# Moving VectorE's LayerNorm rows inside the periods of a fast-algorithm FFN product

## Chip, cores and metric

One Trainium2 chip, all 8 cores. Each core computes one of the 8 batch elements by itself; nothing is exchanged between cores. The metric is the device time in microseconds (us) of the slowest core.

## What is computed

One encoder layer. The mixing sublayer (convolution, windowed attention, memory attention, a gated merge) ends in LayerNorm 1, and a SwiGLU network with LayerNorm 2 follows. Per core the sequence has 2048 tokens of 1024 channels, and the inner width of the network is 2816. What matters here:

```python
def layer_norm(x, g, b):
    mu = jnp.mean(xf, axis=-1, keepdims=True)
    var = jnp.mean(jnp.square(xf - mu), axis=-1, keepdims=True)
    return ((xf - mu) * lax.rsqrt(var + LN_EPS)) * g + b

x = layer_norm(DEEPNORM_ALPHA * x + merged @ w_o, ln1_g, ln1_b)
gate, up = jnp.split(x @ w_ffn_in, 2, axis=-1)
ffn = (jax.nn.silu(gate) * up) @ w_ffn_out
return layer_norm(DEEPNORM_ALPHA * x + ffn, ln2_g, ln2_b)
```

## The kernel before

Tokens go in 16 blocks of 128 (`tb`), in two passes of 8 blocks (`P`). Every engine runs its instructions in the order in which the program issues them, and waits for other engines by semaphore. There is no planner: the order is the order of the Python calls.

**The first FFN product** runs over 44 units (22 for each pass): `u` even is a gate unit (128 columns of the gate half), `u` odd the up unit that is multiplied with the gate of the unit before. Each unit is a 2 by 2 block product by a scheme with seven block products in place of eight. `f1_period(cur, prev)` is one period: it interleaves the early products of unit `cur` with the late ones of unit `prev`. A full period is seven products of four matmuls (`prod`, all recorded at L233), which I number:

1. of `cur`, copied out of PSUM by ACT (`t1`, L1163)
2. of `prev`, copied by ACT (`t3`, L1163)
3. of `cur`, added by DVE into `t1` (`c11`, L1166); if `cur` is an up unit, POOL then multiplies it with its gate (L1173)
4. of `prev`, added by DVE into `t3` (`c22`, L1166)
5. of `cur`, copied by ACT (`tu`)
6. of `prev`; if `prev` is a gate unit, ACT takes two SiLUs (L1169), else DVE (L1174) and POOL (L1173) take products
7. of `prev`, accumulated on top of product 4 in the same bank, which therefore waits until `c22` has read it; DVE then adds it into another buffer (`c12`, L1166)

At the end of a period DVE folds the weights of unit `cur + 2` (`fold_w1`, three instructions at L806 to L808), which SP loaded at the period's start (`load_w1`, 512 KB, from a cache in HBM), as soon as product 7 of the period before was done with the buffer.

**LayerNorm 1 of blocks 8 to 15** is interleaved with the first pass. `d_chain(t)` issues, for a handful of blocks in different stages: the store of the row that `d_Y` made one call before (`y_pend`, SP, 512 KB), transposes of block `t-4` on PE (`d_Tpe`, L1109), the sum of squares and small statistics of block `t` on ACT (L1023, L1082 to L1084) and POOL (L1086, L1037), the copy of the transposes by ACT, and DVE's two rows: `d_C(t-2)` (scale and offset, L1045) and `d_Y(t-1)` (centre and gain, L1041), each one pass over 128x1024 floats. It is called behind every even period `u` from 0 to 18, with `t = 10 + u//2`; rows of C come up to `t = 17`, rows of Y up to `t = 16`.

From `u = 8` on, POOL issues two loads of the second product's weights behind each period (`load_w2`, cast from float to bf16).

**The second FFN product** (`f2_block`) runs a block of 128 tokens at a time; behind each block comes LayerNorm 2: DVE's addition of the residual (L1284), ACT's sum of squares, three small DVE instructions, DVE's rows `ln_center` (L1041) and `ln_scale` (L1045), the store of the output on SP, and on SP again `load_hb(tb + 3)`, which waits until that store has landed. Block 7 is the last of the first pass; the early products of unit 22 run among its matmuls, and the periods 23 to 43 follow it.

Of the kernel before, what the change touches and what calls it, by code (L numbers as in the profile page):

```python
# [97 lines left out]
def _build(plan):  # L98
# [27 lines left out]
    out_d = nc.dram_tensor("out", [T, D], F32, kind="ExternalOutput").ap()  # L126
# [9 lines left out]
    sp = Eng(nc, nc.sync, "sp", plan)  # L136
# [8 lines left out]
    def dma(e, out, in_, slot, deps=()):  # L145
        e.wait(deps)
        e.eng.dma_start(out=out, in_=in_).then_inc(slot.sem, 16)  # L147
        slot.count += 16
        return slot.tok()
# [31 lines left out]
    rs16 = nc.alloc_sbuf_tensor("rs16", [128, 32], F32)  # L181
# [794 lines left out]
    e_state = {}  # L976
# [63 lines left out]
    def ln_center(buf, tab, k, deps):  # L1040
        return dve.run(lambda: nc.vector.scalar_tensor_tensor(  # L1041
            out=buf, in0=buf, scalar=mvt[:, k % 4, 0:1], in1=tab, op0=ALU.subtract, op1=ALU.mult), deps)

    def ln_scale(buf, dst, rs, tab, deps):
        return dve.run(lambda: nc.vector.scalar_tensor_tensor(  # L1045
            out=dst, in0=buf, scalar=rs, in1=tab, op0=ALU.mult, op1=ALU.add), deps)
# [42 lines left out]
    y_pend = []  # L1089
# [25 lines left out]
    def d_Tev(tb):  # L1115
        bT, t_tr = d_state.pop(("tr", tb))
        t_x1T[tb] = act.run(lambda: nc.scalar.copy(
            x1T[:, tb // 8, (tb // 4) % 2, :, (tb % 4) * 128:(tb % 4 + 1) * 128], psb[:, bT, :].rearrange("p (a b) -> p a b", a=8)), [t_tr])
        banks.release(bT, t_x1T[tb])
# [45 lines left out]
    def plus(buf, b, deps):  # L1165
        return dve.run(lambda: nc.vector.tensor_tensor(out=buf, in0=buf, in1=ps[:, b, :], op=ALU.add), deps)  # L1166
# [6 lines left out]
            return pool.run(lambda: nc.gpsimd.tensor_tensor(out=dst, in0=up, in1=gate, op=ALU.mult), deps)  # L1173
        return dve.run(lambda: nc.vector.tensor_tensor(out=dst, in0=up, in1=gate, op=ALU.mult), deps)  # L1174

    def f1_period(cur, prev, fill=lambda: None, part=None):
        new = cur is not None and cur not in unit
        if cur is not None:
            load_w1(cur + 2)
            P, i, up, W, A11, A12, A21, A22 = f1_operands(cur)  # L1180
            n = i % 2
            free = t_free.setdefault(("u",) if up else ("g", n), {})
        if new:
            s = unit[cur] = {"T": TU if up else [TG[n], TG[2 + n], TG[4], TG[5]]}
            s["x"], dx = banks.alloc(1)
            t = prod(s["x"], W, 0, A11, True, [dx, w1_tok[cur], t_x1T[8 * P:8 * P + 8]])
            s["t1"] = grab(s["T"][0], s["x"], [t, free.get("11"), tg0])
        if prev is not None:
            q = unit[prev]
            Pq, iq, upq, Wq, A11q, A12q, S3q, A22q = f1_operands(prev)  # L1190
            g = unit[prev - 1] if upq else None
            j1, j2 = actT[2 * iq], actT[2 * iq + 1]
            sa = sa_tok[Pq]
            t = prod(q["x"], Wq, 5, S3q, False, [q["tu"], sa[3]])
            q["t3"] = grab(q["T"][2], q["x"], [t, c_free[upq]])
        fill()
        if new:
            y, dy = banks.alloc(1)
            t = prod(y, W, 3, A12, True, [dy])
            s["c11"] = plus(s["T"][0], y, [t, s["t1"]])  # L1200
            banks.release(y, s["c11"])
            if up:
                gg = unit[cur - 1]
                a_tok[2 * i, 0] = times(actT[2 * i][:, 0:512], s["T"][0], gg["T"][0], [s["c11"], gg["g11"], e_state["dep"]])
                free["11"] = a_tok[2 * i, 0]
                t_free["g", n]["11"] = a_tok[2 * i, 0]
        if silu12:
            silu12.pop()()
        if prev is not None:
            z, dz = banks.alloc(1)  # L1210
            t = prod(z, Wq, 4, SA[:, 0], True, [dz, sa[1]])
            q["c22"] = plus(q["T"][2], z, [t, q["t3"]])
            fill()
        if part == "head":
            return
        if cur is not None and "tu" not in unit[cur]:
            s = unit[cur]
            t = prod(s["x"], W, 6, SA[:, 1], False, [s["t1"], sa_tok[P][2]])
            s["tu"] = grab(s["T"][1], s["x"], [t, free.get("12"), tg0])
            if not up:  # L1220
                s["g11"] = silu(s["T"][0], s["T"][0], [s["c11"]])
        if prev is not None:
            t = prod(q["x"], Wq, 1, A22q, False, [q["t3"]])
            if not upq:
                q["g22"] = silu(q["T"][2], q["T"][2], [q["c22"]])
                q["g21"] = silu(q["T"][3], ps[:, q["x"], :], [t, d_free[0]])
                banks.release(q["x"], q["g21"])
            else:
                a_tok[2 * iq, 1] = d_free[0] = times(j1[:, 512:1024], ps[:, q["x"], :], g["T"][3], [t, g["g21"], e_state["dep"]], dve)
                banks.release(q["x"], d_free[0])  # L1230
            fill()
            t = prod(z, Wq, 2, SA[:, 2], False, [q["c22"], sa[4]])
            w1_free[prev % 4] = [t]
            e_state["mm"] = t
            q["c12"] = plus(q["T"][1], z, [t, q["tu"]])
            banks.release(z, q["c12"])
            if not upq:
                def later12():
                    q["g12"] = silu(q["T"][1], q["T"][1], [q["c12"]])
                silu12.append(later12)  # L1240
            else:
                a_tok[2 * iq + 1, 1] = times(j2[:, 512:1024], q["T"][2], g["T"][2], [q["c22"], g["g22"], e_state["dep"]])
                c_free[0] = c_free[1] = a_tok[2 * iq + 1, 1]
                a_tok[2 * iq + 1, 0] = times(j2[:, 0:512], q["T"][1], g["T"][1], [q["c12"], g["g12"]])
                t_free["u",]["12"] = t_free["g", iq % 2]["12"] = a_tok[2 * iq + 1, 0]
        if cur is not None and part is None:
            fold_w1(cur + 2)
# [4 lines left out]
    def load_hb(tb):  # L1252
        if tb < 16:
            r = tb % 3
            hb_tok[tb] = dma(sp, HB[r], y_d[tb * 128:(tb + 1) * 128, :], hb_slot[r], [x1_st[tb], hb_free[r]])
# [24 lines left out]
    def f2_block(tb, hooks={}):  # L1280
        r = tb % 3
        bO, tk = f2_mm(tb, hooks)
        xb = HB[r]
        t_h = dve.run(lambda: nc.vector.scalar_tensor_tensor(  # L1284
            out=xb, in0=xb, scalar=ALPHA, in1=bank2(bO), op0=ALU.mult, op1=ALU.add,
            accum_out=hsum[:, 1, tb:tb + 1]), [tk, hb_x[tb]])
        banks.release(bO, t_h, 2)
        t_st2 = ln_stats(xb, [t_h], tb)
        t3 = ln_tiny(t_st2, tb, hsum[:, 1, tb:tb + 1], 0)
        t_rs2 = ln_rstd(t3, tb, rs16[:, 16 + tb:17 + tb])  # L1290
        t_y = ln_center(xb, ln2t[0], tb, [t3, e_state["ln2"]])
        t_ln = ln_scale(xb, xb, rs16[:, 16 + tb:17 + tb], ln2t[1], [t_rs2, t_y])
        hb_free[r] = [dma(sp, out_d[tb * 128:(tb + 1) * 128, :], xb, s_out[r], [t_ln])]
        load_hb(tb + 3)

    hb_x = {}

# [1 line left out]
        if tb < 16:  # L1299
            hb_x[tb] = ln_scale_ap(HB[tb % 3], rs16[:, tb:tb + 1], ln1t[:, 1, :], [hb_tok[tb], d_state["rs", tb]])  # L1300

    def d_chain(t, lo, hi):
        while y_pend:
            y_pend.pop(0)()
        if lo <= t - 4 < hi:
            d_Tpe(t - 4)
        if lo <= t < hi:
            d_S(t)
            d_small(t)
        if lo <= t - 4 < hi:  # L1310
            d_Tev(t - 4)
        if lo <= t - 2 < hi:
            d_C(t - 2)
        if lo <= t - 1 < hi:
            d_Y(t - 1)

    def f1_begin(u, second=False):
        f1_period(u, None, part="second" if second else "head")
# [15 lines left out]
            d_chain(tb - 6, 8, 16)  # L1334
    w2_order = list(range(22))
    for u in range(22):
        f1_period(u, u - 1 if u else None)
        if u % 2 == 0 and u < 20:
            d_chain(10 + u // 2, 8, 16)
        if u >= 8:  # L1340
            for _ in range(2):
                if w2_order:
                    load_w2(w2_order.pop(0))
# [18 lines left out]
    for P in range(2):  # L1362
        if P == 0:
            e_sums(1, [e_state["mm"]])
            for tb in range(3):
                load_hb(tb)
            hb_prep(0)
        for tb in range(8 * P, 8 * P + 8):
            if tb not in (7, 15):
                hb_prep(tb + 1)  # L1370
            f2_block(tb, {24: lambda: f1_begin(22), 8: lambda: f1_begin(22, True)} if tb == 7 else {})
            if tb in (1, 2):
                fold_w1(23 + tb)
        if P == 0:
            for u in range(22, 44):
                f1_period(u, u - 1 if u > 22 else None)
                if u == 32:
                    hb_prep(8)
            f1_drain(43, 8)
# [67 lines left out]
```

How the kernel before makes its waits and increments, by code:

```python
    def wait(self, deps):  # L45
        for tok in _flat(deps):
            if tok[0] == "E":
                _, src, v = tok
                k = id(src)
                if self.seen.get(k, 0) >= v:
                    continue
                self.seen[k] = v
                src.needed.add(v)
                if self.plan is not None:
                    self.eng.wait_ge(src.sem, src.vmap[v])
            else:
                sem, val = tok
                k = id(sem)
                if self.seen.get(k, 0) >= val:
                    continue
                self.eng.wait_ge(sem, val)
                self.seen[k] = val
# [1 line left out]
    def run(self, fn, deps=(), inc=True):  # L64
        self.wait(deps)
        ins = fn()
        if inc:
            self.v += 1
            if self.plan is None or self.v in self.plan[self.name]:
                ins.then_inc(self.sem, 1)
                self.real += 1
                self.vmap[self.v] = self.real
            return ("E", self, self.v)
        return None
# [70 lines left out]
    def dma(e, out, in_, slot, deps=()):  # L145
        e.wait(deps)
        e.eng.dma_start(out=out, in_=in_).then_inc(slot.sem, 16)
        slot.count += 16
        return slot.tok()
```

## Time and profile before

| | us |
|---|---|
| median of 3 runs | 1018.44 (1018.06 to 1021.53) |
| the profiled execution | 1019.49 |
| its span on the slowest core (core 7) | 1018.3 |
| spans of the 8 cores | 1006.7 to 1018.3 |

| engine, slowest core | busy us | share of the span |
|---|---|---|
| PE (matmuls) | 964.3 | 95% |
| DVE | 547.4 | 54% |
| ACT | 408.1 | 40% |
| POOL | 288.9 | 28% |

The shares are averages over stages with different limits. Of the chain of work that ended last, PE holds 85%; what is left to gain is in the gaps between matmuls, and in the stretches where the granted TensorE clock falls to its lower level. Times inside the trace are counted in us from the start of the span.

### The profile page before, as it was taken

The numbers are of one execution on the slowest core, as the hardware profiler recorded it, in microseconds if no ns is written. First come the engines' busy times: TensorE is split into PE (matmuls) and PEld (weight loads), VectorE is DVE, ScalarE is ACT, GpSimd is POOL, SyncE is SP. The second block draws the span as 40 slices with busy tenths as digits, with TensorE's granted clock in tenths as the row PEclk, the third lists the DMA queues.
The fourth block names the chain that finished last, engine by engine and source line by source line (L and its number), as shares of the span: only waits on it lengthen the run. The fifth ranks groups of instructions, "written<-read, shape, count | busy, mean of one in ns | idle before, by whom it ended". The sixth has DMA issues, their size and how long they took to land.

```text
span 1018.3 us, 16359 instructions; the slowest of 8 cores (1006.7 to 1018.3 us)
## 1 busy us (share of the span) xinstructions
PE 964.3 (95%) x5606; PEld 448.6 (44%) x5606; DVE 547.4 (54%) x903; ACT 408.1 (40%) x653; POOL 288.9 (28%) x296
## 2 busy tenths in 40 slices
PE   4999999989899999999999988999999999999996
PEld 1455544534444444444445434444444344444442
DVE  0324575657472222223377777677476477773554
ACT  1135666757462222222343445454222344443221
POOL 3200000202144324323321334443333133333331
PEclk9999999999899999999999999999999999999999
DMA  9996134554249999730084234886433332220222
GB/s 131 167 174 130 23 93 105 74 108 74 54 69 142 132 150 145 118 124 1 1 271 185 75 112 104 187 179 152 145 125 124 105 100 86 84 83 1 83 106 81
DMA packets 39392, 112.11 MB, mean 110 GB/s; under 512 B 4944, under 2 KB 16856, under 8 KB 38192
## 3 DMA queue, kind: packets, MB, share of 16 engines
q0 software_dynamic: 11104, 41.16, 27.6%
q1 hardware_dynamic: 28208, 69.91, 21.7%
q8 instruction: 47, 0.77, 0.3%
q14 instruction: 33, 0.27, 0.1%
HBM read 132.49 MB, written 30.47 MB: 160 GB/s over the span
## 4 chain that ended last, share of the span: by engine, by line
PE 85%; DMA 6%; DVE 4%; issue 2%; ACT 1%; SPq 1%; POOL 1%; DVEq 0%; ACTq 0%; POOLq 0%
PE ps L233 84%; DMA arena<-xt 2%; DMA arena<-w_out 2%; DVE arena L1166 1%; DVE arena L1041 1%; DMA arena<-u_scratch 1%; SPq L147 1%; DMA arena<-w_bf_cache 1%; PE ps L1109 1%; POOL arena L147 1%; DVE arena L1045 0%; ACT arena L597 0%; PE ps L688 0%; DVE arena L807 0%; ACT arena L645 0%
## 5 line engine op out<-in xcount | busy, mean ns | idle before, releaser
L233 PE MATMUL ps<-arena 128*128 128x512 bf16 (+5 forms) x5196 | 948.6, 362 | 43.6 <-DVE arena L1166 15.9
L233 PEld LDWEIGHTS ps<-arena 128*128 128x128 bf16 (+2 forms) x5196 | 428.5, 98 | 546.4 <-issue 92.8
L837 DVE SCALAR_TENSOR_TENSOR arena<-arena,ps 128x512 f32<-128x512 f32 x96 | 65.8, 686 | 144.3 <-PE ps L233 140.3
L1173 POOL TENSOR_TENSOR arena<-arena 128x512 bf16<-128x512 f32 x66 | 88.6, 1342 | 178.2 <-DVE arena L1166 172.0
L1163 ACT COPY arena<-ps 128x512 f32<-128x512 f32 x132 | 77.1, 586 | 136.8 <-PE ps L233 136.0
L816 ACT ACTIVATE arena<-ps,bgate_sb 128x512 f32<-128x512 f32 x96 | 65.8, 687 | 164.4 <-PE ps L233 164.4
L1166 DVE TENSOR_TENSOR arena<-arena,ps 128x512 f32<-128x512 f32 x132 | 88.8, 686 | 57.9 <-PE ps L233 54.1
L844 POOL TENSOR_TENSOR arena<-arena 128x512 f32<-128x512 f32 x32 | 40.8, 1275 | 123.0 <-DVE arena L837 123.0
L1023 ACT ACTIVATE arena<-arena 128x1024 bf16<-128x1024 f32 x32 | 33.7, 1054 | 92.2 <-DVE arena L1284 81.0
L147 POOL DMA_DIRECT2D arena<-w_g x21 | 11.3, 544 | 170.0 <-PE ps L233 168.8
L849 POOL TENSOR_TENSOR arena<-arena 128x512 bf16<-128x512 f32 x32 | 42.3, 1322 | 43.2 <-DVE arena L837 41.6
L1045 DVE SCALAR_TENSOR_TENSOR arena<-arena,rs 128x1024 bf16<-128x1024 f32 (+1 forms) x32 | 50.5, 1579 | 1.8
L645 ACT ACTIVATE arena<-ps 128x1024 bf16<-128x1024 f32 x46 | 46.6, 1025 | 12.2 <-PE ps L233 11.9
L1050 POOL TENSOR_TENSOR arena<-arena 128x1024 f32<-128x1024 f32 x16 | 41.1, 2574 | 28.4 <-ACT arena L1049 28.3
L648 DVE TENSOR_TENSOR arena<-arena 128x1024 bf16<-128x1024 bf16 x46 | 33.8, 737 | 28.3 <-ACT arena L645 28.2
L1169 ACT ACTIVATE arena<-arena 128x512 f32<-128x512 f32 x66 | 41.7, 632 | 16.8 <-DVE arena L1166 16.8
L1037 POOL TENSOR_TENSOR rs<-mvt,eps_t 128x1 f32<-128x1 f32 x32 | 21.5, 673 | 77.7 <-DVE mvt L1033 75.4
L1041 DVE SCALAR_TENSOR_TENSOR arena<-arena,mvt 128x1024 f32<-128x1024 f32 x32 | 41.3, 1290 | 1.7 <-DVE mvt L1033 0.2
L1284 DVE SCALAR_TENSOR_TENSOR arena<-arena,ps 128x1024 f32<-128x1024 f32 x16 | 19.5, 1219 | 40.1 <-PE ps L233 33.5
L807 DVE TENSOR_TENSOR arena<-arena 128x512 bf16<-128x512 bf16 x44 | 37.5, 852 | 4.6
L352 ACT CAST arena<-ps 128x512 bf16<-128x512 f32 (+1 forms) x32 | 18.3, 571 | 38.9 <-PE ps L233 38.9
L806 DVE TENSOR_TENSOR arena<-arena 128x1024 bf16<-128x1024 bf16 x44 | 31.9, 726 | 2.6 <-DMA arena<-w_bf_cache 2.6
(103 smaller groups left out, 449.8 us busy)
## 6 DMA issues: line engine op xcount, KB each, us to landing
arena<-w_bf_cache SPq DMA_DIRECT2D x44, 512.0 KB, 3.9
arena<-u_scratch SPq DMA_DIRECT2D x64, 135.0 KB, 4.0
arena<-x SPq DMA_DIRECT2D x16, 512.0 KB, 10.5
y_scratch<-arena SPq DMA_DIRECT2D x16, 512.0 KB, 6.3
arena<-y_scratch SPq DMA_DIRECT2D x16, 512.0 KB, 3.6
out<-arena SPq DMA_DIRECT2D x16, 512.0 KB, 2.6
arena<-w_f POOLq DMA_DIRECT2D x22, 256.0 KB, 7.1
arena<-w_g POOLq DMA_DIRECT2D x9, 512.0 KB, 13.0
```

The costliest lines, as they stand in the source:

```text
L233: return pe.run(lambda: nc.tensor.matmul(out, lhsT, rhs, start=start, stop=stop, skip_group_check=onto), deps, inc)
L645: t_p = act.run(lambda: nc.scalar.activation(flat, bank2(b), AF.Exp, scale=0.125), [tk, PTw_free[rp], btab["t"]])
L816: t = act.run(lambda: nc.scalar.activation(gb[r], ps[:, bk, :], AF.Tanh, bias=bgate[:, b * 8 + dc:b * 8 + dc + 1], scale=0.5), [tk, gb_fre ...
L837: t_y = dve.run(lambda: nc.vector.scalar_tensor_tensor(out=gb[r], in0=gb[r], scalar=1.0, in1=ps[:, bk, :], op0=ALU.add, op1=ALU.mult), [tk ...
L849: t_mg[dp, tt, dci] = pool.run(lambda: nc.gpsimd.tensor_tensor(out=merged[dp][:, dci, tt * 512:(tt + 1) * 512], in0=gb[r0], in1=gb[r], op= ...
L1041: return dve.run(lambda: nc.vector.scalar_tensor_tensor(out=buf, in0=buf, scalar=mvt[:, k % 4, 0:1], in1=tab, op0=ALU.subtract, op1=ALU.mu ...
L1045: return dve.run(lambda: nc.vector.scalar_tensor_tensor(out=dst, in0=buf, scalar=rs, in1=tab, op0=ALU.mult, op1=ALU.add), deps)
L1050: return pool.run(lambda: nc.gpsimd.tensor_tensor(out=buf, in0=buf, in1=tab, op=ALU.add), [t])
L1163: return act.run(lambda: nc.scalar.copy(buf, ps[:, b, :]), deps)
L1166: return dve.run(lambda: nc.vector.tensor_tensor(out=buf, in0=buf, in1=ps[:, b, :], op=ALU.add), deps)
L1169: return act.run(lambda: nc.scalar.activation(buf, src, AF.Silu), deps)
L1173: return pool.run(lambda: nc.gpsimd.tensor_tensor(out=dst, in0=up, in1=gate, op=ALU.mult), deps)
```

## The change

The rows and the rest of `d_chain` become two functions, `d_rows` and `d_lines`. In the first pass `d_rows(t)` is called inside the odd periods (`cur` an up unit, `prev` a gate unit), right behind `c22`, through a new argument `extra` of `f1_period`; `d_lines(t)` is called behind the same odd period. Nothing is called behind even periods any more, so the transposes, the statistics and the store move by one period as well; the store of a row is now issued behind the period in which the row is made. `d_chain` elsewhere is as it was. For block 7, the centre and scale rows of LayerNorm 2, the store of its output and `load_hb(10)` are returned as a function and issued behind `c22` of period 23. No instruction is added or taken away.

```diff
-    def f1_period(cur, prev, fill=lambda: None, part=None):
+    def f1_period(cur, prev, fill=lambda: None, part=None, extra=lambda: None):
...
             q["c22"] = plus(q["T"][2], z, [t, q["t3"]])
+            extra()
             fill()
...
-        t_y = ln_center(xb, ln2t[0], tb, [t3, e_state["ln2"]])
-        t_ln = ln_scale(xb, xb, rs16[:, 16 + tb:17 + tb], ln2t[1], [t_rs2, t_y])
-        hb_free[r] = [dma(sp, out_d[tb * 128:(tb + 1) * 128, :], xb, s_out[r], [t_ln])]
-        load_hb(tb + 3)
+
+        def rows():
+            t_y = ln_center(xb, ln2t[0], tb, [t3, e_state["ln2"]])
+            t_ln = ln_scale(xb, xb, rs16[:, 16 + tb:17 + tb], ln2t[1], [t_rs2, t_y])
+            hb_free[r] = [dma(sp, out_d[tb * 128:(tb + 1) * 128, :], xb, s_out[r], [t_ln])]
+            load_hb(tb + 3)
+        if tb == 7:
+            return rows
+        rows()
...
-    def d_chain(t, lo, hi):
+    def d_lines(t, lo, hi):
         while y_pend:
             y_pend.pop(0)()
         if lo <= t - 4 < hi:
...
             d_Tev(t - 4)
+
+    def d_rows(t, lo, hi):
+        while y_pend:
+            y_pend.pop(0)()
         if lo <= t - 2 < hi:
             d_C(t - 2)
         if lo <= t - 1 < hi:
             d_Y(t - 1)
+
+    def d_chain(t, lo, hi):
+        d_lines(t, lo, hi)
+        d_rows(t, lo, hi)
...
-        f1_period(u, u - 1 if u else None)
-        if u % 2 == 0 and u < 20:
-            d_chain(10 + u // 2, 8, 16)
+        t = 10 + u // 2
+        f1_period(u, u - 1 if u else None, extra=(lambda: d_rows(t, 8, 16)) if u % 2 else lambda: None)
+        if u % 2:
+            d_lines(t, 8, 16)
...
-                f1_period(u, u - 1 if u > 22 else None)
+                f1_period(u, u - 1 if u > 22 else None, extra=rows7 if u == 23 else lambda: None)
```

## Rows read from the trace of the kernel before

**Rows 1.** PE's waits, whole span: us in total, times, longest.
```profile
PE ps L233 <- DVE arena L1166: 15.9, 10, 2.4
```

**Rows 2.** PE's timeline, first pass: start, length, instructions, [idle before <- releaser].
```profile
604.26 7.07 PE L233 MATMUL ps<-arena 128*128 128x512 bf16 x32 [1.45 <-DVE arena L1166]
...
648.00 8.75 PE L233 MATMUL ps<-arena 128*128 128x512 bf16 x32 [2.40 <-DVE arena L1166]
```

**Rows 3.** PE's timeline, second pass.
```profile
804.57 62.28 PE L233 MATMUL ps<-arena 128*128 128x512 bf16 x280 [2.40 <-DVE arena L1166]
868.30 140.88 PE L233 MATMUL ps<-arena 128*128 128x512 bf16 x652 [1.45 <-DVE arena L1166]
```

**Rows 4.** Busy time by stretch; after the engines: granted clock, DMA share, GB/s.
```profile
648.00:656.75 8.75, 8.75 (x35) 3.71 (x36) 4.21 (x7) 3.88 (x7) 3.04 (x4) 0.80 1.01 202
...
804.50:809.00 4.50, 4.43 (x14) 1.69 (x15) 0.69 (x1) 1.84 (x4) 0.80 (x1) 0.64 0.54 198
```

**Rows 5.** DVE's timeline, end of period 4 to the end of period 6.
```profile
597.90 0.68 DVE L806 TENSOR_TENSOR arena<-arena 128x1024 bf16<-128x1024 bf16 x1
...
600.45 1.28 DVE L1045 SCALAR_TENSOR_TENSOR arena<-arena,rs 128x1024 bf16<-128x1024 f32 x1
601.64 1.28 DVE L1041 SCALAR_TENSOR_TENSOR arena<-arena,mvt 128x1024 f32<-128x1024 f32 x1
602.84 1.28 DVE L1166 TENSOR_TENSOR arena<-arena,ps 128x512 f32<-128x512 f32 x2
...
606.00 0.68 DVE L806 TENSOR_TENSOR arena<-arena 128x1024 bf16<-128x1024 bf16 x1
...
607.32 0.43 DVE L808 TENSOR_TENSOR arena<-arena 128x512 bf16<-128x512 bf16 x1
608.05 0.69 DVE L1166 TENSOR_TENSOR arena<-arena,ps 128x512 f32<-128x512 f32 x1 [0.31 <-PE ps L233]
...
611.44 0.69 DVE L1166 TENSOR_TENSOR arena<-arena,ps 128x512 f32<-128x512 f32 x1 [0.17 <-PE ps L233]
```

**Rows 6.** DVE's timeline, second pass: `c11`/`c22` of period 23, product 6 of 24 and 26.
```profile
803.14 1.28 DVE L1166 TENSOR_TENSOR arena<-arena,ps 128x512 f32<-128x512 f32 x2
...
812.57 0.69 DVE L1174 TENSOR_TENSOR arena<-ps,arena 128x512 bf16<-128x512 f32 x1 [0.97 <-PE ps L233]
...
824.65 0.69 DVE L1174 TENSOR_TENSOR arena<-ps,arena 128x512 bf16<-128x512 f32 x1 [0.97 <-PE ps L233]
```

**Rows 7.** The chain that ended last, piece by piece: start, length, what (transposes behind period 4).
```profile
597.19 0.45 PE ps L1109 x8
```

**Rows 8.** POOL's timeline, periods 4 and 5.
```profile
600.19 0.74 POOL L1037 TENSOR_TENSOR rs<-mvt,eps_t 128x1 f32<-128x1 f32 x1
603.66 1.27 POOL L1173 TENSOR_TENSOR arena<-arena 128x512 bf16<-128x512 f32 x1 [2.73 <-DVE arena L1166]
```

**Rows 9.** Timeline of POOL and DVE at a block of the second product.
```profile
738.65 2.97 POOL L1050 TENSOR_TENSOR arena<-arena 128x1024 f32<-128x1024 f32 x1
739.53 3.18 DVE L1045 SCALAR_TENSOR_TENSOR arena<-arena,rs 128x1024 f32<-128x1024 f32 x1
```

**Rows 10.** ACT's timeline: `t1` and `t3` of period 5 behind the lines.
```profile
598.89 1.20 ACT L1163 COPY arena<-ps 128x512 f32<-128x512 f32 x2
```

**Rows 11.** DMA issues around 605.6: out<-in, queue, count, KB, median us to landing.
```profile
y_scratch<-arena SPq DMA_DIRECT2D x1, 512.0 KB, 4.9
```

**Rows 12.** DMA issues from 633.9 to 634.5 (behind period 9).
```profile
arena<-w_f POOLq DMA_DIRECT2D x2, 256.0 KB, 8.1
arena<-w_bf_cache SPq DMA_DIRECT2D x1, 512.0 KB, 8.4
y_scratch<-arena SPq DMA_DIRECT2D x1, 512.0 KB, 10.3
```

**Rows 13.** SP's timeline at the start of the second pass: start, length, what it issues.
```profile
803.30 0.34 SPq L147 DMA_DIRECT2D out<-arena  x1
...
806.42 19.38 SPq L147 DMA_DIRECT2D arena<-w_bf_cache  x4
```

**Rows 14.** DMA issues from 803 to 807.
```profile
arena<-w_bf_cache SPq DMA_DIRECT2D x1, 512.0 KB, 4.5
```

More of the change, by code:

```diff
@@ L1370, in _build @@
                 hb_prep(tb + 1)
-            f2_block(tb, {24: lambda: f1_begin(22), 8: lambda: f1_begin(22, True)} if tb == 7 else {})
+            rows7 = f2_block(tb, {24: lambda: f1_begin(22), 8: lambda: f1_begin(22, True)} if tb == 7 else {})
             if tb in (1, 2):
```

## The prediction

> **What bounds the kernel now.** I read PE's waits first. Behind the input loads at the start, the largest entry is the wait for DVE's additions L1166: ten stalls, 15.9 us [rows 1]. PE's timeline places them: two in the second pass, of 2.40 and 1.45 us [rows 3], and the other eight, 12.05 us together, in the first pass, one in each odd period up to 15; two of them stand as rows [rows 2]. The reader is to see that the stall comes ahead of a piece that begins with product 7, which needs `c22`. DVE's timeline says why: behind an even period come the fold, then C, then Y, and only then `c11` and `c22` back to back [rows 5]. DVE isn't full there, its queue is merely in the wrong order. Last, the clock: two stretches behind a stall of 2.40 us show a granted clock of 0.80 and 0.64, so partly the lower level, 1.2 GHz, where full stretches have 2.4 [rows 4]. The piece at 648.00 takes 8.75 us where the same 32 matmuls take 7.07 at 604.26 [rows 2]: 1.7 us. The piece at 804.57 runs 280 matmuls in 62.28, at the pace of the next piece (140.88 for 652) they would take 60.5: 1.7 again [rows 3].
>
> **A clock for a pair of periods.** Product 6 of periods 24 and 26 lie 12.08 us apart [rows 6]: a period is 6.04, a product 0.863. The transposes add 0.45 to a pair [rows 7]. I count from the first matmul of an odd period: its product 7 is due at 6 x 0.863 = 5.18, the even period begins at 6.49 (with the transposes now behind the odd one), the next odd one at 12.53. Period 6 begins at 604.26 + 0.863 = 605.12, and there DVE isn't late: `c11` starts 2.93 and `c12` 6.32 into it [rows 2, 5]. When DVE is late, `c11` and `c22` run back to back and product 7 starts 604.26 - 602.84 = 1.42 behind the start of `c11` [rows 2, 5].
>
> **First pass, what goes.** With the rows out of its way, the fold of an even period starts at 6.49 + 6.32 + 0.61 = 13.42 (a following DVE instruction starts some 0.6 behind an addition, 1.28 for two and 0.69 for one). It lasts 600.45 - 597.90 = 2.55 [rows 5], so `c11` of the odd period starts at 15.97 - 12.53 = 3.44 and product 7 may go at 4.86, due 5.18. The stall is gone, 0.32 to spare. That removes 12.05 us, and the 1.7 of clock behind the stall at 648.
>
> **First pass, what comes.** In the odd period the rows stand between `c22` and `c12`. `c11` at 3.44, `c22` at 4.04, C wants to start at 4.65. But POOL's gate product follows `c11` by 603.66 - 602.84 = 0.82 and lasts 1.27 [rows 5, 8]: it holds 4.26 to 5.53. C reads two operands from SBUF, and the trace shows what that costs: an L1045 issued at 739.53, while POOL worked until 741.62, ended at 742.71, 1.09 behind POOL [rows 9]. So C ends at 6.62, Y (1.19 from start to start [rows 5]) starts at 6.54 and ends at 7.82, and `c12`, due 6.32, starts at 7.74. Queued behind it on DVE is the fold, 8.35 to 10.10 at 1.75 (606.00 to 607.32 + 0.43 [rows 5]); `c11` of the even period starts 3.61 into it, product 7 may go at 5.03, due 5.18. No stall, 0.15 to spare. Nobody else waits soon for `c12`: its SiLU on ACT comes a period later.
>
> What could eat 0.15 is POOL's small statistics (0.74 for the last, [rows 8]), which now meet the odd fold. That instruction ran at 600.19 while C started at 600.45, and C still took 1.28 [rows 5, 8]. Bounds: 0, or 0.74 - 0.15 = 0.6 in each of 7 pairs, 4.1. A gain is out, since PE has no further wait to lose. I take 0.5 in all, near the row.
>
> The Trainium skill, SBUF — State Buffer, section Who interferes with whom, has this as a rule: a DVE instruction with two SBUF inputs and a GpSimd instruction that reads SBUF exclude each other for their whole length. It speaks against the place chosen here. For C the trace agrees (ended 1.09 behind POOL [rows 9]); for the small instruction it doesn't show it (C 1.28 beside it). By the rule to the letter the 4.1 would be paid.
>
> ACT's lines, the copy of the transposes and POOL's small work move behind the odd period. There ACT has two SiLUs behind product 6 instead of one, so `t1` of the even period starts perhaps 1 us late (today it runs back to back with `t3` at 598.89 [rows 10], some 0.4 late). It ends about 2.7 into the period, ahead of `c11` at 3.61: nothing, and 0.9 to spare before it would cost.
>
> **SP's queue.** Today the store of a row follows `load_w1`, a period after the row was made. Now it stands in front of the even period's `load_w1`, and SP waits in it for Y: store at about 8.0, load at 8.4, second on the same queue. Who waits is the even fold at 13.42. A second transfer landed 4.9 behind its issue before period 8 [rows 11]: 13.3, just in time, nothing. From period 8 on POOL loads weights too, and there a second transfer took 10.3 [rows 12]: 18.7. From landing to product 7 it takes the fold and the two additions, 1.75 + 1.42 = 3.17; due is 12.53 + 5.18 = 17.71, so the stall is landing minus 14.54. That is 0 to 4.2 us for each of the three stores of periods 9, 11 and 13, up to 12.5. POOL's pair was issued together with the load then [rows 12]; now it comes about 1 us behind the store. I take 0.6 each, 1.8, near the lower end.
>
> **Second pass.** In period 23 `c11` and `c22` start at 803.14 behind Y and C (2.6 together). Without these `c11` starts at about 800.5, product 7 may go at 801.95, due 804.57 - 2.40 = 802.17 [rows 3, 6]. So 2.40 and the 1.7 of clock go. But the rows now wait for POOL's gate product (801.35 to 802.62 by the 0.82 and 1.27 above): Y ends at 803.71, C at 805.1, and the output's store goes out 1.9 later than its 803.30 [rows 13]. Behind it on SP stands `load_hb(10)`, which waits for its landing, and behind that the weights of unit 26, which landed at 806.42 + 4.5 = 810.9 [rows 13, 14]: now 812.8. Plus 3.17 makes 816.0 for product 7 of period 25, due 803.03 + 6.04 + 5.18 = 814.25. **A new stall of 1.75 us** (1.0 without the lock, if the store is 1.1 late). The clock: the stall of 1.45 at 868.30 left the pace at 0.216 for a matmul [rows 3], so I take nothing, at most 1.7. The stall at 868.30 lies ten periods on and stays.
>
> **Sum.** First pass 12.05 + 1.7 - 0.5 - 1.8 = 11.45; second pass 2.40 + 1.7 - 1.75 = 2.35; together 13.8. Against the profiled execution, 1019.49 (span 1018.3 and 1.2 around it), that gives 1005.7. The median of the runs is 1.05 lower, 1018.44, and by it 1004.6. I forecast 1005.
>
> **Rivals.**
> - *The load lands late.* The swap on SP decides. For it: the three pairs with POOL's loads, at 8.4 and 10.3 a transfer [rows 12], and that each stall makes the next Y, store and load later. Against it: POOL's pair is issued later than today. At 3 to 4.2 us each, 9 to 12.5 in place of 1.8: 1013 to 1016; at half that price, 1009 to 1010.
> - *The lock costs all of it.* 0.6 to 1 us in seven even periods because POOL's product and small work block C, Y and the fold in turn: 4 to 7 in place of 0.5, 1008.5 to 1012.
> - *No price at all.* The load on time, the new stall at 1.0: 12.05 + 1.7 + 4.1 - 1.0 = 16.85 gone, 1002.6, by the median 1001.6.
> - *Slower.* The store ahead of the load is late in all seven pairs, with 10.3 from issue to landing also before period 8: 7 x 4.2 = 29 against 11.45 + 1.8 + 2.35 = 15.6 won: about 1033. It turns slower when the mean landing passes 14.54 + 15.6 / 7 = 16.8, 8.4 behind the load's issue. Against it speak the 4.9 without POOL's loads [rows 11].
>
> That the order isn't as said is no rival: each queue runs in program order.
>
> **How the numbers follow.** Forecast, 1003 to 1008: 0.57. Load late: 0.17, a third of it above 1013. Lock: 0.10. No price: 0.13. Slower: 0.03. The range from 1000.5 to 1012 leaves out the slower case, the upper part of the late loads and a little below. About 0.5%, 5 us, is what a measurement can tell from no change: faster than 1013.3 has 0.91, within 0.5% 0.06, slower 0.03.
>
> **What the profile will show.** PE's waits for L1166 should fall from ten to two or three: the one of 1.45 late in the second pass, a new one in period 25, perhaps small ones in periods 11, 13 and 15. DVE's timeline should have `c11`, `c22`, C, Y, `c12` in odd periods with C stretched to about 2 us; a C of 1.28 proves my lock wrong. The fold of even periods 10, 12 and 14 idle before L806, ended by the weights' DMA, would show the late load; stalls in even periods would show the lock. The granted clock should have no dip in the first pass. If PE's waits vanish and the time doesn't fall by as much, another core or the start of the program sets the end, and my sum on core 7 was the wrong one.

## The result

The changed kernel takes 1008.11 us, the median of five executions (1005.87 to 1011.95), beside 1019.43 for the kernel before in the same comparison. Times here and below leave out executions in which the cores of a die show a lower granted clock than the others and run longer (one of 1089.21 for this kernel). The ratio is 0.989, 95% interval 0.986 to 0.992, so about 11 us less. Forecast were 1005 and a range of 1000.5 to 1012. The profiled execution took 1010.17 with a span of 1009.1 on its slowest core, which now is core 1, not core 7.

PE's waits for DVE on that core, to be set beside [rows 1] (us in total, times, longest), and its timeline, beside [rows 2, 3] (start, length, instructions, idle before and what ended it):

```profile
PE ps L233 <- DVE arena L1166: 7.2, 4, 2.3
```

```profile
640.87 1.72 PE L233 MATMUL ps<-arena 128*128 128x512 bf16 x4 [2.26 <-DVE arena L1166]
669.73 1.02 PE L233 MATMUL ps<-arena 128*128 128x512 bf16 x4 [1.96 <-DVE arena L1166]
809.14 48.51 PE L233 MATMUL ps<-arena 128*128 128x512 bf16 x224 [1.51 <-DVE arena L1166]
859.11 140.88 PE L233 MATMUL ps<-arena 128*128 128x512 bf16 x652 [1.46 <-DVE arena L1166]
```

Ten waits have become four. All eight of the first pass are gone from their old places; two new ones stand in periods 11 and 15, one in period 25 of the second pass, and the last is the old one of [rows 3], which nothing touched.

The kernel's time is that of the slowest core, and which core that is depends mostly on the start (in eight of the eleven profiled executions it is the core that starts the stage last): DVE's last L1070 (the residual addition of the first sublayer) comes between 561.7 and 569.6 us on the eight cores before, and between 562.1 and 571.6 after. What the change touches lies behind it. So I count a **stage** on every core: from the start of DVE's last L1070 to the start of its addition behind block 8 (the ninth of its line, L1284 before, L1285 after; the line number moves with the edits), from DVE's timeline of each core. Its mean over the eight cores is **371.1 us before (368.9 to 373.3) and 360.8 after (358.1 to 362.1)**: 10.3 less. On core 7, on which the prediction was worked out, it is 373.3 and 360.2: 13.0 less, where 13.8 were forecast. Its first and last line on that core, before and then after:

```profile
569.61 1.22 DVE L1070 SCALAR_TENSOR_TENSOR arena<-arena,ps 128x1024 f32<-128x1024 f32 x1 [3.61 <-PE ps L233]
942.89 1.22 DVE L1284 SCALAR_TENSOR_TENSOR arena<-arena,ps 128x1024 f32<-128x1024 f32 x1 [5.65 <-PE ps L233]
```

```profile
563.54 1.22 DVE L1070 SCALAR_TENSOR_TENSOR arena<-arena,ps 128x1024 f32<-128x1024 f32 x1 [3.61 <-PE ps L233]
923.78 1.22 DVE L1285 SCALAR_TENSOR_TENSOR arena<-arena,ps 128x1024 f32<-128x1024 f32 x1 [5.65 <-PE ps L233]
```

DVE's timeline of periods 3 and 4 on core 1, beside [rows 5], and POOL's of the same time, beside [rows 8]:

```profile
586.76 1.28 DVE L1166 TENSOR_TENSOR arena<-arena,ps 128x512 f32<-128x512 f32 x2
587.96 2.05 DVE L1045 SCALAR_TENSOR_TENSOR arena<-arena,rs 128x1024 bf16<-128x1024 f32 x1
589.93 1.27 DVE L1041 SCALAR_TENSOR_TENSOR arena<-arena,mvt 128x1024 f32<-128x1024 f32 x1
591.12 0.68 DVE L1166 TENSOR_TENSOR arena<-arena,ps 128x512 f32<-128x512 f32 x1
591.72 0.68 DVE L806 TENSOR_TENSOR arena<-arena 128x1024 bf16<-128x1024 bf16 x1
592.51 0.42 DVE L807 TENSOR_TENSOR arena<-arena 128x512 bf16<-128x512 bf16 x1
...
593.38 1.28 DVE L1166 TENSOR_TENSOR arena<-arena,ps 128x512 f32<-128x512 f32 x2
```

```profile
587.65 1.27 POOL L1173 TENSOR_TENSOR arena<-arena 128x512 bf16<-128x512 f32 x1 [1.61 <-DVE arena L1166]
591.15 0.19 POOL L1086 TENSOR_TENSOR mvt<-mvt 128x1 f32<-128x1 f32 x1 [2.22 <-ACT mvt L1084]
591.48 0.55 POOL L1037 TENSOR_TENSOR rs<-mvt,eps_t 128x1 f32<-128x1 f32 x1
```

The reader is to see the order `c11`, `c22`, C, Y, `c12`, fold, with no idle time between, and C stretched to 2.05 beside POOL's product of 587.65 to 588.92. POOL's two small instructions run beside `c12` and the fold and stretch nothing.

Where the new waits come from stands one period earlier on DVE, and in the DMA issues (out<-in, queue, count, KB, us to landing) from 628.5 to 629.4:

```profile
633.53 0.69 DVE L1166 TENSOR_TENSOR arena<-arena,ps 128x512 f32<-128x512 f32 x1 [0.17 <-PE ps L233]
637.77 0.69 DVE L806 TENSOR_TENSOR arena<-arena 128x1024 bf16<-128x1024 bf16 x1 [3.55 <-DMA arena<-w_bf_cache]
```

```profile
y_scratch<-arena SPq DMA_DIRECT2D x1, 512.0 KB, 3.0
arena<-w_bf_cache SPq DMA_DIRECT2D x1, 512.0 KB, 8.4
```

The fold of period 10 stands idle for 3.55 us for weights whose load was issued behind the store and took 8.4. In period 25 it is the same picture. DVE and SP at the start of the second pass, beside [rows 6] and [rows 13], and the DMA issues from 798 to 802.2, beside [rows 14]:

```profile
793.82 1.29 DVE L1166 TENSOR_TENSOR arena<-arena,ps 128x512 f32<-128x512 f32 x2
795.03 2.04 DVE L1041 SCALAR_TENSOR_TENSOR arena<-arena,mvt 128x1024 f32<-128x1024 f32 x1
797.17 1.28 DVE L1045 SCALAR_TENSOR_TENSOR arena<-arena,rs 128x1024 f32<-128x1024 f32 x1
...
806.05 0.69 DVE L806 TENSOR_TENSOR arena<-arena 128x1024 bf16<-128x1024 bf16 x1 [2.79 <-DMA arena<-w_bf_cache]
```

```profile
798.53 0.34 SPq L147 DMA_DIRECT2D out<-arena  x1
801.24 0.32 SPq L147 DMA_DIRECT2D arena<-y_scratch  x1
801.65 8.91 SPq L147 DMA_DIRECT2D arena<-w_bf_cache  x3
```

```profile
out<-arena SPq DMA_DIRECT2D x1, 512.0 KB, 2.6
arena<-y_scratch SPq DMA_DIRECT2D x1, 512.0 KB, 3.4
arena<-w_bf_cache SPq DMA_DIRECT2D x1, 512.0 KB, 4.3
```

The weights of unit 26 leave at 801.65 behind store and reload, and land 4.3 later, at 805.95; the fold starts at 806.05.

### The profile page after: what moved, and what is told of

Same layout as the page of the kernel before. It is cut to its first block, busy times and chain, and to the rows that moved or that the text cites. A ratio compares the mean times of both kernels' runs of the same rounds, so it can differ in the third digit from the quotient of the medians.

```text
span 1009.1 us, 16357 instructions; the slowest of 8 cores (995.7 to 1009.1 us)
## 1 busy us (share of the span) xinstructions
PE 962.5 (95%) x5606; PEld 449.3 (45%) x5606; DVE 549.9 (54%) x903; ACT 407.7 (40%) x653; POOL 286.3 (28%) x296
## 4 chain that ended last, share of the span: by engine, by line
PE 84%; DMA 8%; DVE 3%; issue 2%; ACT 1%; SPq 1%; POOL 0%; DVEq 0%; ACTq 0%; POOLq 0%
PE ps L233 83%; DMA arena<-w_out 2%; DMA arena<-w_bf_cache 2%; DMA arena<-w_q 1%; DMA arena<-xt 1%; SPq L147 1%; DMA arena<-u_scratch 1%; DMA gexp_scratch<-arena 1%; PE ps L1109 1%; DVE arena L1166 1%; DVE arena L1045 0%; DVE arena L1041 0%; POOL arena L147 0%; ACT arena L597 0%; PE ps L688 0%
## 5 line engine op out<-in xcount | busy, mean ns | idle before, releaser
L1045 DVE SCALAR_TENSOR_TENSOR arena<-arena,rs 128x1024 bf16<-128x1024 f32 (+1 forms) x32 | 56.1, 1752 | 1.7
L1037 POOL TENSOR_TENSOR rs<-mvt,eps_t 128x1 f32<-128x1 f32 x32 | 19.9, 622 | 79.2 <-DVE mvt L1033 77.0
L1285 DVE SCALAR_TENSOR_TENSOR arena<-arena,ps 128x1024 f32<-128x1024 f32 x16 | 19.5, 1218 | 40.0 <-PE ps L233 34.0
L807 DVE TENSOR_TENSOR arena<-arena 128x512 bf16<-128x512 bf16 x44 | 35.1, 798 | 4.9 <-DVE arena L806 0.5
L806 DVE TENSOR_TENSOR arena<-arena 128x1024 bf16<-128x1024 bf16 x44 | 32.3, 734 | 9.8 <-DMA arena<-w_bf_cache 9.8
```

The costliest lines, as they stand in the source:

```text
L1045: return dve.run(lambda: nc.vector.scalar_tensor_tensor(out=dst, in0=buf, scalar=rs, in1=tab, op0=ALU.mult, op1=ALU.add), deps)
```

## The experiments

The theory after the result: DVE's order is right now, and what is left are two late loads, both late because of their place in SP's queue: (a) in the first pass the store stands ahead of the even period's load while POOL's weight loads are in flight; (b) at the start of the second pass block 7's store and reload stand ahead of the load for unit 26. The rival: DVE is crowded between `c22` and `c12` and by the exclusion with POOL, and would make PE wait whatever SP does.

The table has, for each kernel, the stage (mean of eight cores, with the lowest and highest) and PE's idle time in it (mean; gaps above 0.15 us, read from PE's timeline of each core). The expectations stand as they were written ahead of the runs. Each core has its own waits, so one execution's stage mean is uncertain by about 0.1 to 0.7 us (the spread of its eight cores divided by the root of eight).

| kernel | stage, us | PE idle in it, us |
|---|---|---|
| before | 371.07 (368.94 to 373.28) | 15.64 |
| the change | 360.81 (358.14 to 362.10) | 6.24 |
| e1, block 7 only | 370.11 (368.39 to 371.31) | 15.30 |
| e10, first pass only | 361.85 (358.51 to 365.36) | 6.78 |
| e2, block 7's DMAs behind | 357.91 (355.18 to 360.70) | 3.78 |
| e3, store behind the load | 357.74 (356.16 to 360.79) | 3.87 |
| e4, POOL's loads later | 357.74 (357.00 to 359.40) | 4.04 |
| e5, e2 and e3 | 355.11 (354.66 to 355.69) | 1.96 |
| e7, rows in even periods | 366.00 (365.58 to 368.25) | 11.18 |
| e8, POOL's product behind the rows | 357.58 (356.78 to 359.34) | 3.99 |
| e9, e5 and e8 | 355.02 (354.58 to 355.46) | 1.91 |

**The two parts alone (e1, e10).** e1 keeps the second part of the change:

```diff
-        t = 10 + u // 2
-        f1_period(u, u - 1 if u else None, extra=(lambda: d_rows(t, 8, 16)) if u % 2 else lambda: None)
-        if u % 2:
-            d_lines(t, 8, 16)
+        f1_period(u, u - 1 if u else None)
+        if u % 2 == 0 and u < 20:
+            d_chain(10 + u // 2, 8, 16)
```

> Only the second part of the change: block 7's rows, store and reload move behind c22 of period 23, the first pass is as before. I count the stage from DVE's last residual addition of the first sublayer to its addition behind block 8, mean of the eight cores: 371.1 us before, 360.8 with the whole change. My theory: the part is worth little by itself, since the weights of unit 26 now stand on SP behind the later store and the reload; the wait of 2.40 at the start of the pass goes, with the clock drop on four of eight cores, and a new wait of 1.5 to 3.4 (2.1 in the mean) stands in period 25. Stage 369.5 to 370.5. Rival: the new wait comes from DVE being crowded by the first pass's part, so here it is absent and the stage falls by the whole 2.4 and the clock, to 367.8.

Measured: 370.11, 1.0 below before. The wait of 2.40 is gone on every core, and one of 1.74 to 2.05 (mean 1.87) stands in period 25 on every core. On its slowest core the fold of unit 26 and the wait behind it read:

```profile
812.87 0.69 DVE L806 TENSOR_TENSOR arena<-arena 128x1024 bf16<-128x1024 bf16 x1 [3.03 <-DMA arena<-w_bf_cache]
```

```profile
815.96 48.51 PE L233 MATMUL ps<-arena 128*128 128x512 bf16 x224 [1.74 <-DVE arena L1166]
```

The rival is out: with a first pass like that of the kernel before, the wait is there all the same. Block 7's part gives back most of what it wins. e10 is the other half:

```diff
-        if tb == 7:
-            return rows
         rows()
...
-                f1_period(u, u - 1 if u > 22 else None, extra=rows7 if u == 23 else lambda: None)
+                f1_period(u, u - 1 if u > 22 else None, extra=lambda: None)
```

> Only the first part of the change: rows inside odd periods, block 7 as before. Theory (the parts don't act on each other): the stage falls from 371.1 by what the whole change gives, 10.3, less the 1.0 of block 7's part alone: 361 to 362.5, with one wait of 2.40 at the start of the second pass on every core, none in period 25, and the same late folds 10 to 14. Rival (the first part crowds SP or DVE so that block 7's part gains more or less than alone): outside of that.

Measured: 361.85, with 2.40 at the start of the second pass on every core and no wait in period 25. Within the uncertainty the parts add: 1.0 and 9.2 against 10.3 together.

**The second late load (e2).** Block 7's rows stay in period 23, its two DMAs go behind period 24 and so behind the load for unit 26:

```diff
-            hb_free[r] = [dma(sp, out_d[tb * 128:(tb + 1) * 128, :], xb, s_out[r], [t_ln])]
-            load_hb(tb + 3)
+
+            def tail():
+                hb_free[r] = [dma(sp, out_d[tb * 128:(tb + 1) * 128, :], xb, s_out[r], [t_ln])]
+                load_hb(tb + 3)
+            return tail
...
+                if u == 24:
+                    tail7.pop()()
```

> The whole change, but block 7's store and the reload of block 10 are issued behind period 24, so that the load of unit 26's weights stands ahead of them on SP. Theory (SP's order makes the wait of period 25): DVE's idle time before the fold of unit 26, 2.8 to 4.7 us, vanishes, the wait of 1.5 to 3.4 with it, and the stage falls from 360.8 to 358.3 to 358.8. Rival (the rows behind c22 and POOL's lock hold DVE up): the wait stays above 1 us.

Measured: 357.91, 2.9 below the change. No core waits in period 25 (0 of 8; 1.5 to 3.4 us on 8 of 8 with the change). The period behind 24 on its slowest core, beside the 2.79 us of idle time above:

```profile
799.93 0.69 DVE L1166 TENSOR_TENSOR arena<-arena,ps 128x512 f32<-128x512 f32 x1 [0.17 <-PE ps L233]
800.54 0.69 DVE L806 TENSOR_TENSOR arena<-arena 128x1024 bf16<-128x1024 bf16 x1
```

The gain is 0.4 more than was expected; the late folds of the first pass, which this kernel shares with the change, cost it 2.3 us of waits a core in this execution where the change had 2.7.

**The first late load (e3, e4).** e3 issues the store behind the even period, so that the load is ahead of it again:

```diff
-    def d_lines(t, lo, hi):
-        while y_pend:
+    def d_lines(t, lo, hi, stores=True):
+        while stores and y_pend:
...
         if u % 2:
-            d_lines(t, 8, 16)
+            d_lines(t, 8, 16, False)
+        else:
+            while y_pend:
+                y_pend.pop(0)()
```

> The whole change, but in the first pass the store of a row is issued behind the even period, so that SP has the load of the weights ahead of it, as before the change. Theory (the store in front of the load makes the folds of periods 10 to 14 late): the idle times of 2 to 3.9 us before these folds fall to the 0 to 1.75 of the kernel before, PE's waits in periods 11 to 15 fall from 2.7 us a core to under 1, with the clock drops behind them; stage 357.5 to 358.5. Rival (DVE has no slack left, whatever the order on SP; or POOL's weight loads alone do it): waits of 2 to 3 us a core stay.

Measured: 357.74, 3.1 below the change. The waits of periods 11 to 15 are at most 0.50 us on any core, 0.14 in the mean (1.3 to 4.2, mean 2.6, with the change). On its slowest core only the waits of periods 17 (0.39), 25 and 33 are left:

```profile
PE ps L233 <- DVE arena L1166: 5.0, 3, 3.1
```

The load behind period 13 takes 7.8 to 8.9 us here as well (7.4 to 8.7 with the change), but it is issued 3.0 us behind the start of `c11` in place of 4.9, in the mean of the cores. So the store's part is to hold back the issue of the load, not to make the load long. e4 leaves the store where the change has it and moves POOL's loads:

```diff
-        if u >= 8:
-            for _ in range(2):
+        if u >= 14:
+            for _ in range(3):
```

> The whole change, but POOL's loads of the second product's weights begin behind period 14 with three a period, in place of behind period 8 with two. The store stays in front of the load. Theory (it takes both, the store in front and POOL's loads beside it): the folds of periods 10 to 14 don't wait, as those of periods 2 to 8 don't; stage 357.5 to 358.5 unless the denser loads make later folds wait, which would show as idle time before folds 16 to 19. Rival (the order on SP alone is enough): waits of 1.5 to 2.5 in periods 11 to 15 stay.

Measured: 357.74. No core waits in periods 11 to 15, and the folds of periods 10 and 12 don't wait; those of 16 to 20, now beside denser loads, wait up to 2.1 us, which costs PE 0.2 to 1.2 a core. The loads behind periods 9, 11 and 13 are issued as late as with the change (4.9 behind the start of `c11`), but take 4.0 to 5.6 us. So it takes both, the store in front and POOL's loads beside it; either taken away is enough. With the store in front but no loads of POOL a load of the same kernel, the change, took 4.7 us; this issue is from 616 to 617 on core 1:

```profile
y_scratch<-arena SPq DMA_DIRECT2D x1, 512.0 KB, 3.0
arena<-w_bf_cache SPq DMA_DIRECT2D x1, 512.0 KB, 4.7
```

**Both (e5).**

> Both reorderings on SP at once: the store of a row behind the even period, and block 7's store and reload behind period 24. Theory (the two late loads are all that is left of DVE's waits, and independent): the gains add, stage 360.8 - 3.1 - 2.9 = 354.8; PE's waits for DVE fall to the one of 1.46 late in the second pass and less than 0.7 a core besides; against the kernel before, 371.1 - 354.8 = 16 us or 0.984. Rival (with one wait gone the next is late, the usual end of such repairs): less than half of the second gain comes, stage above 356.3.

Measured: 355.11, and PE's waits for DVE are down to 1.5 to 2.6 a core. The gains of 2.9 and 3.1 add to 5.7. Little takes their place: beside the wait of 1.46, three cores have one of 0.75 to 0.88 in period 15 and four one of 0.39 in period 17, together up to 1.14 on a core, a little more than the 0.7 expected. The waits on its slowest core:

```profile
PE ps L233 <- DVE arena L1166: 2.3, 2, 1.5
```

It takes 1001.94 us (median of four executions), a ratio of **0.983** to the kernel before, interval 0.9817 to 0.9843. The kernel of the change has 0.986 to 0.992, so this version beats both.

**The place in the pair (e7).** The same rows in the even periods, where `prev` is an up unit:

```diff
-        f1_period(u, u - 1 if u else None, extra=(lambda: d_rows(t, 8, 16)) if u % 2 else lambda: None)
-        if u % 2:
+        f1_period(u, u - 1 if u else None, extra=(lambda: d_rows(t, 8, 16)) if u % 2 == 0 and u < 20 else lambda: None)
+        if u == 0:
+            d_rows(t, 8, 16)
+        if u % 2 == 0 and u < 20:
             d_lines(t, 8, 16)
```

> The rows behind c22 of the even periods (cur a gate unit, prev an up unit), where DVE also has the product behind product 6; lines and store behind the even period too. All else as in the change. Theory (DVE has 0.15 to 0.3 us to spare in a pair, and the place matters since the fold of an even period is the long one, 2.55 against 1.75): c12 and the fold end 1 to 2 us later than in odd periods, product 7 of the odd period waits 0.3 to 1.5 us in eight pairs, and the late loads come on top: stage 364 to 371. Rival (any place behind c22 does, only the late loads cost): stage 360 to 362.

Measured: 366.00, 5.2 above the change; 0.9955 of the kernel before, interval 0.994 to 0.9971. DVE, POOL and PE on its slowest core:

```profile
596.01 1.28 DVE L1045 SCALAR_TENSOR_TENSOR arena<-arena,rs 128x1024 bf16<-128x1024 f32 x1
597.21 2.30 DVE L1041 SCALAR_TENSOR_TENSOR arena<-arena,mvt 128x1024 f32<-128x1024 f32 x1
599.43 0.68 DVE L1174 TENSOR_TENSOR arena<-ps,arena 128x512 bf16<-128x512 f32 x1
...
601.41 1.30 DVE L807 TENSOR_TENSOR arena<-arena 128x512 bf16<-128x512 bf16 x1
...
603.16 1.28 DVE L1166 TENSOR_TENSOR arena<-arena,ps 128x512 f32<-128x512 f32 x2
```

```profile
596.30 2.13 POOL L1173 TENSOR_TENSOR arena<-arena 128x512 bf16<-128x512 f32 x1 [4.87 <-DVE arena L1166]
600.91 1.53 POOL L1173 TENSOR_TENSOR arena<-arena 128x512 bf16<-128x512 f32 x1 [2.48 <-ACT arena L1163]
```

```profile
600.25 3.61 PE L233 MATMUL ps<-arena 128*128 128x512 bf16 x16 [0.26 <-DVE arena L1174]
604.58 7.07 PE L233 MATMUL ps<-arena 128*128 128x512 bf16 x32 [0.72 <-DVE arena L1166]
```

Here C starts first and holds off POOL's product (2.13 in place of 1.27), which then holds off Y (2.30 in place of 1.28). L1174 is late behind them, and PE waits for it, 0.26 us, which I hadn't foreseen; the long fold makes `c11` and `c22` late, 0.72. The even fold is long by the same exclusion: its L807 takes 1.30 beside POOL's product of 600.91 to 602.44, where the odd fold's takes 0.42 with POOL's product out of its way. The two waits are about 1 us in each of the five pairs from period 4 on; the first two pairs have 1.36 and 1.58. The second half of my expectation, waits for late weights on top, did not come: in the first pass the folds stand idle for weights for at most 1.13 us, and no wait of PE above 0.15 us follows. The one in period 25, 1.67 to 2.65, is there on every core, as with the change. The place does matter.

**POOL's product (e8, e9).** The gate product of an odd period waits for Y:

```diff
+                def gate11(dep):
+                    a_tok[2 * i, 0] = times(actT[2 * i][:, 0:512], s["T"][0], gg["T"][0],
+                                            [s["c11"], gg["g11"], e_state["dep"], dep])
...
-            extra()
+            dep = extra()
+            if new and up:
+                gate11(dep)
```

> The whole change, but POOL's gate product of an odd period waits for the last row, so that DVE's rows find POOL idle. Theory (POOL's product holds C off, each for its whole length): C takes 1.28 in place of 2.05, the store and the load behind it go out 0.8 earlier, the folds of periods 10 to 14 wait 0.8 less, PE's waits there fall from 2.7 us a core to about 1.4; POOL's product now meets the odd fold and stretches one of its instructions. Stage 358.5 to 360. Rival (what is saved at C is lost at the fold, or the load's time doesn't follow the store): stage 360.5 or more.

Measured: 357.58, a better result than expected. On its slowest core C takes 1.28, and one instruction of the odd fold is stretched instead:

```profile
590.48 1.45 DVE L806 TENSOR_TENSOR arena<-arena 128x1024 bf16<-128x1024 bf16 x1
...
599.81 1.28 DVE L1045 SCALAR_TENSOR_TENSOR arena<-arena,rs 128x1024 bf16<-128x1024 f32 x1
```

The exclusion of C and POOL's product is shown by that: the same instruction, 2.05 with POOL's product running and 1.28 without. The waits of periods 11 to 15 are gone on seven cores (1.70 on the eighth). Two things add up, and the traces of the eight cores show both. The load leaves 0.8 us earlier (4.2 in place of 4.9 behind the start of `c11`). And it takes less, in the mean 4.7, 5.3 and 6.9 us behind periods 9, 11 and 13 in place of 5.7, 5.8 and 8.1, while POOL's pair, issued behind its later product, leaves 2.4 us behind the load in periods 9 and 11 in place of 0.2 to 0.3. That the later pair is what shortens the load is likely, but no run changes it alone.

> Both reorderings on SP together with POOL's product behind the last row. Stage 355.1 with the two reorderings alone. Theory (the product's place matters through the store in front of the load only, and that is gone already): nothing more to gain but the two or three waits of 0.75 to 0.88 behind fold 14; stage 354.5 to 355.2. Rival (C's lock costs by itself, through the crowded DVE): 353.5 to 354.3.

Measured: 355.02, and 1001.44 us (median of three executions), ratio 0.9833 (0.9786 to 0.988). With the store out of the way POOL's product has nothing more to give; the rival, a cost of the exclusion by itself, is out.

## Why the prediction was right, point by point

**The old stalls are gone.** Yes, all of them, on all eight cores: eight in the first pass and the one of 2.40 (12.05 + 2.40 on core 7).

**The clock for a pair.** From the start of `c11` the prediction has C 1.21, Y 3.10, `c12` 4.30 and the next `c11` 6.66 us later. The lines above give 1.20, 3.17, 4.36 and 6.62. No stall follows from it before POOL's loads begin but one of 0.31 on a single core: the margins of 0.15 and 0.32 held.

**The exclusion of C and POOL.** Predicted 1.97 for C, measured 2.05; e8 shows the cause. POOL's small work: predicted between 0 and 4.1, taken as 0.5; it cost nothing (0.19 and 0.55 beside `c12` and L806 of 0.68; L806 stays at 0.68 in all 48 odd folds that L1037 meets on the eight cores). So the Trainium skill's rule (SBUF — State Buffer, Who interferes with whom), that a DVE instruction with two SBUF inputs and a GpSimd one that reads SBUF shut each other out for the whole length, is borne out for the 128x512 product. For the 128x1 instructions no effect shows.

**SP's queue in the first pass.** The step is right (store in front of the load, late from period 8 on, through POOL's loads), and so is the time of issue: the load leaves 4.93 us behind the start of `c11`, 8.37 on the prediction's clock, where it has 8.4. The size isn't: 1.8 us taken, 2.6 measured as the mean of the cores, with single waits up to 2.57. The prices that it has for a transfer in second place, 4.9 and 10.3, are those of a store [rows 11, 12]; a load there took 3.7 to 5.2 us before POOL's loads begin and 4.4 to 8.7 beside them. Three equal prices of 0.6 were wrong too: periods 11, 13 and 15 have 0.48, 0.17 and 1.91. I looked at how far POOL's pair comes behind the store. What goes with a long load in the runs is POOL's earlier loads, still in flight when it is issued: behind period 13 there are two to four of them on every core, and the load takes 7.4 to 8.7 us. These are the lines of core 1, POOL's from 655 to 656.5 and SP's from 657.5 to 658.5:

```profile
arena<-w_f POOLq DMA_DIRECT2D x2, 256.0 KB, 8.2
```

```profile
y_scratch<-arena SPq DMA_DIRECT2D x1, 512.0 KB, 7.5
arena<-w_bf_cache SPq DMA_DIRECT2D x1, 512.0 KB, 8.3
```

**SP's queue in the second pass.** A new stall of 1.75 in period 25 was predicted; 1.51 to 3.39 were measured, mean 2.10. e2 shows the cause.

**The clock.** I took nothing for the new stalls. On five of the eight cores the granted clock fell once, behind a wait of 1.96 to 3.39 us; this is core 1 behind the wait of 2.26, with the clock behind the engines' columns, beside [rows 4]:

```profile
640.90:645.00 4.10, 4.10 (x18) 2.10 (x19) 4.10 (x4) 3.51 (x9) 2.06 (x4) 0.58 0.18 49
```

At 1.7 us each that is 1.1 in the mean of eight cores, a term of the sum that I had at 0.

**The core.** The sum was made on the slowest core of one execution, and that was the one core of eight with two falls of the clock. The others had one or none, seven in all, 1.5 us a core, where I counted 3.4. Over eight cores the account reads: PE's waits 15.64 to 6.24, 9.4 less; the clock 1.5 to 1.1, 0.4 less; 9.8 of the 10.3 measured; the other 0.5 stays open. So the term that was mis-sized most is the clock, 3.4 taken and 0.4 measured in the mean. The forecast of 13.8 was for core 7, which gave 13.0: 11.0 from the waits and 1.7 from the clock. That it came so close there is partly luck, since the waits of periods 11 to 15 are 2.0 on core 7 and anything from 1.3 to 4.2 on the others. Since mostly the start decides which core ends last, the kernel's time should follow the mean of the cores more than the worst.

**The chances.** The time, 1008.1, came out in the forecast's direction, just above its 1003 to 1008 and below the 1009 to 1010 of the late load at half price. The late loads are there, but nearer to the forecast's price than to the rival's: 2.6 us of waits, about 3.4 with the four falls of the clock behind them, beside 1.8 taken and 4.5 to 6.2 at half price. Most of what is missing is the clock.

## What to carry to other kernels

When work is moved to a better place on one engine, its DMAs move too: in an in-order queue a store that waits for its data holds up every load behind it, and here that gave back 6 of the 16 us which the same move wins with the DMAs left behind. Place a long row between two instructions that the matmuls don't wait for soon, and look up what POOL is running at that time, since the two can shut each other out (C 2.05 in place of 1.28). And cost a term on all cores, not on the slowest of one execution, where losses that come by chance are collected.

## What was not expected of the hardware

A load's time depends on what another queue has in flight when it is issued. The same 512 KB behind the same store took 4.7 us at 616.54 and 8.4 at 629.28 on core 1. POOL's next pair, issued 0.23 us behind the second of these, doesn't explain it: on all eight cores that pair comes 0.23 to 0.24 us behind. On the four on which POOL's pair before it had landed, the load takes 4.4 to 5.0 us; on the other four it takes 4.5 to 8.4.

The granted clock fell in e3 on four cores in the first pass with no wait of PE above 0.15 us ahead of it. Core 5 of e3, where PE is busy throughout:

```profile
630.00:634.90 4.90, 4.90 (x20) 2.00 (x19) 3.81 (x6) 2.06 (x4) 3.47 (x4) 0.81 0.96 170
```

This is another fall than the one behind the waits. The four cores are 4 to 7, the whole of one die, and the granted clock is 0.81 for about 5 us (about 0.9 us lost on each), neither the full 2.4 GHz nor the lower level. Cores of the same die show it once more around 520 us in e1 to e4, which ran on one chip; the other kernels don't show it. What sets it off is left open.

Of the falls to the lower level, waits of 1.96 to 2.55 us were followed by one on some cores and not on others (1.96 on core 7 and on core 1 of the change; 2.55 on core 1 of e1, none behind 2.57 on core 0 of the change), so the wait before it alone doesn't tell. What does is left open.
